# Quartered products for the 16- and 32-row tiles of a pooling and recurrence decoder layer

## What is computed

```python
def _layer(x, pool_prev, S0, start_pos, prompt, lb, ...):
    h = _rmsnorm(x, g_mix)
    z = h @ w_in                                   # 1024 -> 4608
    u, q, f, v, og, ga, gb = jnp.split(z, offs, axis=-1)
    pooled = _pool_mix(u_cat, pos)                 # trailing means, windows 2/4/8/16
    ya = (grouped(pooled, w_pool) * pool_scale) @ w_a
    qh = silu(q); fg = lb + (1 - lb) * sigmoid(f); kh = 1 - fg; gh = log(fg)
    # gated recurrence, per head: S_t = diag(fg_t) S_{t-1} + kh_t outer v_t, o_t = S_t^T qh_t
    o = _rmsnorm(o, g_onorm) * silu(og)
    yb = o @ w_b
    m = sigmoid(ga) * ya + sigmoid(gb) * yb
    x = x + m @ w_out
    h2 = _rmsnorm(x, g_mlp)
    x = x + jnp.square(relu(h2 @ w_up)) @ w_down   # 1024 -> 4096 -> 1024
# and y = _rmsnorm(x, g_final); 16 meta tokens stand ahead of each prompt and are dropped from y
```

## Time and profile before

| | |
|---|---|
| median of 3 runs | 899.56 us (899.15 to 900.22) |
| profiled execution: its time, and its span on the slowest core | 899.98 us, 898.4 us |
| spans of the eight cores | 894.7 to 898.4 us |
| mean granted TensorE clock | 0.996 to 0.999 |
| TensorE matmuls busy | 866.9 us, 96% of the span |
| VectorE, ScalarE, GpSimd busy | 418.2, 354.4, 122.1 us |

### The profile page before, as it was taken

The page is one execution under the profiler, slowest core; times in us unless marked ns, Lnnn a source line. Parts: engine busy times, 40 slices in busy tenths (PEclk is TensorE's granted clock), DMA queues, the critical chain, the costliest instruction groups (busy, mean ns, idle before and its releaser), DMA issues.

```text
span 898.4 us, 14902 instructions; the slowest of 8 cores (894.7 to 898.4 us)
## 1 busy us (share of the span) xinstructions
PE 866.9 (96%) x4864; PEld 449.6 (50%) x4945; DVE 418.2 (47%) x695; ACT 354.4 (39%) x625; POOL 122.1 (14%) x190
## 2 busy tenths in 40 slices
PE   4999999999999999999999999999999999999996
PEld 2667654444444444465444444444444444688443
DVE  4574565777487676754544114441144412234122
ACT  3654536564465627541333313332233312233222
POOL 4113320244004511243000000000000000000000
PEclk9999999999999999999999999999999999999999
DMA  9999952448414768978999042200420011200121
GB/s 173 163 169 197 185 144 102 124 120 192 165 47 136 177 192 177 171 106 121 217 204 181 7 137 80 63 1 24 117 94 0 1 47 48 74 1 1 34 67 67
DMA packets 91463, 97.24 MB, mean 108 GB/s; under 512 B 37725, under 2 KB 72157, under 8 KB 91372
## 3 DMA queue, kind: packets, MB, share of 16 engines
q1 hardware_dynamic: 67404, 65.88, 25.7%
q0 software_dynamic: 23984, 30.41, 23.9%
HBM read 92.35 MB, written 26.11 MB: 132 GB/s over the span
## 4 chain that ended last, share of the span: by engine, by line
PE 86%; DVE 4%; issue 4%; ACT 4%; DMA 1%; POOL 0%; DVEq 0%; ACTq 0%; SPq 0%; POOLq 0%
PE ps L595 48%; PE ps L1357 24%; PE ps L607 8%; ACT arena L573 3%; PE ps L1054 2%; DVE arena L576 1%; DVE arena L676 1%; DVE arena L696 1%; DMA arena<-xp 1%; PE ps L621 1%; PE ps L1246 1%; PE ps L906 0%; PE ps L762 0%; PE ps L779 0%; PE ps L1355 0%
## 5 line engine op out<-in xcount | busy, mean ns | idle before, releaser
L595 PE MATMUL ps<-arena 128*128 128x512 bf16 (+2 forms) x2675 | 489.8, 338 | 7.0 <-ACT arena L573 2.4
L595 PEld LDWEIGHTS ps<-arena 128*128 128x128 bf16 x2720 | 261.0, 98 | 211.9 <-issue 16.0
L573 ACT ACTIVATE arena<-ps 128x512 f32<-128x512 f32 (+7 forms) x318 | 185.8, 597 | 293.7 <-PE ps L595 205.9
L573 ACT ACTIVATE arena<-arena 128x1024 bf16<-128x1024 f32 (+6 forms) x234 | 152.2, 666 | 243.4 <-DVE arena L1371 167.6
L1357 PE MATMUL ps<-arena 128*128 128x512 bf16 x1003 | 220.6, 379 | 1.2 <-issue 0.2
L576 DVE TENSOR_TENSOR arena<-arena 128x512 bf16<-128x512 f32 (+6 forms) x214 | 146.4, 691 | 134.7 <-ACT arena L573 125.6
L1357 PEld LDWEIGHTS ps<-arena 128*128 128x128 bf16 x1024 | 100.0, 98 | 121.4 <-issue 1.3
L576 DVE TENSOR_TENSOR arena<-ps,arena 128x512 f32<-128x512 f32 (+4 forms) x153 | 105.9, 708 | 74.2 <-PE ps L595 17.4
L607 PE MATMUL ps<-arena 128*128 128x512 bf16 (+2 forms) x469 | 106.6, 379 | 0.9 <-issue 0.3
L1371 DVE SCALAR_TENSOR_TENSOR arena<-ps,arena 128x1024 f32<-128x1024 f32 (+2 forms) x18 | 22.0, 1222 | 152.5 <-PE ps L1357 138.2
L576 POOL TENSOR_TENSOR arena<-arena 128x512 f32<-128x512 bf16 (+7 forms) x78 | 77.8, 1004 | 74.7 <-DMA arena<-sth 23.6
(11 more groups left out here) (97 smaller groups left out, 237.1 us busy)
## 6 DMA issues: line engine op xcount, KB each, us to landing
arena<-xp SPq DMA_DIRECT2D x32, 512.0 KB, 6.7
arena<-w_in POOLq DMA_DIRECT2D x9, 1024.0 KB, 20.5
x1d<-arena SPq DMA_DIRECT2D x16, 512.0 KB, 5.2
arena<-w_up POOLq DMA_DIRECT2D x8, 1024.0 KB, 12.7
arena<-x1d SPq DMA_DIRECT2D x16, 512.0 KB, 4.6
y_p<-arena SPq DMA_DIRECT2D x15, 512.0 KB, 2.9
arena<-w_down POOLq DMA_DIRECT2D x5, 1024.0 KB, 25.5
h2d<-arena SPq DMA_DIRECT2D x16, 256.0 KB, 4.6
```

The lines of the kernel that those rows point to most:

```text
L573: P.add("act", lambda h: h.activation(out=out, in_=in_, func=func, **kw), reads=reads, writes=writes)
L595: i = h.matmul(ps[:, bb, 0:m], lhsT=wfn(k), rhs=rfn(k, c, m), start=(k == 0), stop=(k == K - 1))
```

## The change

The three small products go in quarters like the down projection: matmul k writes to partitions 32 (k % 4) and up, so each quarter of the array's columns adds up two of the eight k. The four partial sums then lie in four quarters of the bank's partitions, and VectorE adds them: a copy of the first to SBUF and three additions for v and og, four additions to `X` for the output projection, a copy and three additions for the down projection. ScalarE then reads the sum from SBUF. The down projection's copy by ScalarE and its `sel` matmuls go, and its last steps are no longer put off.

```diff
+        def quarters(lfn, K, rfn, rows, ps_of, nh, wr, rd):
+
+            def mm(h):
+                for k in range(K):
+                    for half in range(nh):
+                        j = 32 * (k % 4)
+                        i = h.matmul(ps_of(half)[j:j + rows], lhsT=lfn(k), rhs=rfn(k, half), start=(k < 4), stop=(k >= K - 4))
+                return i
+            P.add("pe", mm, reads=rd, writes=wr)
...
             def u_tm(blk, t, evac):
                 W = wblk[SLOT[blk]]
                 if t < 0:
-                    tm(lambda k: H[:, k, 0:32], 8, lambda k: W[:, k, :], 32, evac, [bH[4]] + r_w[SLOT[blk]].bufs)
+                    b = banks(1)
+                    quarters(lambda k: H[:, k, 0:32], 8, lambda k, half: W[:, k, :], 32, lambda half: ps[:, b, :], 1, [b_ps[b]], [bH[4]] + r_w[SLOT[blk]].bufs)
+                    for j in range(4):
+                        if j == 0:
+                            P.add("dve", lambda h: h.tensor_copy(out=osq[0:32, :], in_=ps[0:32, b, :]), reads=[b_ps[b]], writes=r_oq.bufs)
+                        else:
+                            tt(osq[0:32, :], ps[32 * j:32 * j + 32, b, :], osq[0:32, :], ALU.add, [b_ps[b]] + r_oq.bufs, r_oq.bufs)
+                    evac(osq[0:32, :], r_oq.bufs)
...
                 X, bX = xi[t]
+                if t == 4:
+                    b = banks(2)
+                    quarters(lambda k: mT[:, k, 512:528], 8, lambda k, hf: wo[:, k, hf * 512:(hf + 1) * 512], 16, lambda hf: ps[:, b + hf, :], 2, b_ps[b:b + 2], r_wo.bufs + r_mT.bufs)
+                    Xv = X[0:16, :].rearrange("p (a n) -> p a n", a=2)
+                    for j in range(4):
+                        tt(Xv, ps[32 * j:32 * j + 16, b:b + 2, :], Xv, ALU.add, b_ps[b:b + 2] + bX, bX)
+                    return
...
                     U(lambda: u_o(t, 0))
-                    U(lambda: u_o(t, 1))
+                    if t < 4:
+                        U(lambda: u_o(t, 1))
...
                 if t == 4:
                     activate(r_cp)
-                    P.add("act", lambda h, b=b: h.activation(out=cp.rearrange("p (a n) -> p a n", a=2), in_=ps[:, b:b + 2, :], func=AF.Copy), reads=[b_ps[b], b_ps[b + 1]], writes=r_cp.bufs)
-
-                    def fin16(out=out, fin=fin):
-                        pb = banks(2)
-
-                        def mm(h):
-                            for half in range(2):
-                                x = h.matmul(ps[0:16, pb + half, :], lhsT=sel, rhs=cp[:, half * 512:(half + 1) * 512], start=True, stop=True)
-                            return x
-                        P.add("pe", mm, reads=r_cp.bufs + [b_pk], writes=[b_ps[pb], b_ps[pb + 1]])
-                        out((0, 1), src=ps[0:16, pb:pb + 2, :], bsrc=[b_ps[pb], b_ps[pb + 1]])
-                        fin(((0, 1024),))
-                    pend.append(fin16)
+                    cv = cp[0:16, :].rearrange("p (a n) -> p a n", a=2)
+                    for j in range(4):
+                        if j == 0:
+                            P.add("dve", lambda h, b=b: h.tensor_copy(out=cv, in_=ps[0:16, b:b + 2, :]), reads=[b_ps[b], b_ps[b + 1]], writes=r_cp.bufs)
+                        else:
+                            tt(cv, ps[32 * j:32 * j + 16, b:b + 2, :], cv, ALU.add, [b_ps[b], b_ps[b + 1]] + r_cp.bufs, r_cp.bufs)
+                    out((0, 1), src=cv, bsrc=r_cp.bufs)
+                    fin(((0, 1024),))
```

More of the change, by code:

```diff
@@ L333, in build_program @@
         gon = pk[:, 316:317]
-        sel = pk[:, 320:336]
         ident_b, (b_idb,) = keep(128, BF16)
@@ L1328, in down @@
             seq = [0, 4, 1, 2, 3] if g == 3 else [0, 1, 2, 3]
-            pend = []
             for n, t in enumerate(seq):
@@ L1360, in down @@
                 x1load(rows_of.index((g, t)) + 1)
-                while pend:
-                    pend.pop(0)()
                 halves = [[Buf("half")], [Buf("half")]]
```

## The result

The changed kernel takes 910.61 us (median of five runs) against 899.93 for the kernel before in the same runs: 1.0116 of it, 95% interval 1.0102 to 1.0129, so 9.2 to 11.6 us slower. 908.9 had been forecast, with 905.0 to 911.8 as the range.

The account below looks back on a forecast made before the run. TensorE, busy 866.9 of 898.4 us, was taken to bound the kernel. Terms 6.4 + 3.0 + 0 - 1.8 + 1.7 = +9.3 us gave 909.3, or 908.9 for the median; range 905.0 to 911.8.

Parts of the forecast that it names:

- the clock term: TensorE's waits at `u_v` and `u_og`: one half-rate stretch of 3.4 us counted in full, +1.7 us, bounds 0 and 3.4.
- place 1: `u_v(-1)`: additions behind `prep_scan(1)` make TensorE wait for the bank and ScalarE for the sum; +6.4 us, bounds 5.7 to 6.9.
- TensorE has no slack to absorb a stall: Whole kernel: TensorE is busy 866.9 of 898.4 us, so any stall or saving on it should show in the total.
- the second wait that I had announced: Before the first `u_u`: TensorE waits about 2 us for ScalarE, after its wait of 5 to 6 us for VectorE.
- Place 2: `u_og(-1)`: additions delay `prep_q(3)`, which the first recurrence tile's products need; +3.0 us, bounds 2.3 to 3.5.
- Place 3: Output projection, tile 4: 2.3 us saved, then lost waiting ahead of `up(0)`'s third unit; 0, bounds -0.5 to +0.5.
- Place 4: Down projection: `sel` matmuls leave TensorE's path and the next tile's 64 matmuls hide the additions; -1.8 us.
- a clock that stays down for longer than one such stretch: Sign the prediction is wrong: half rate lasting longer than one 3.4 us stretch behind TensorE's waits.
- both clock falls in full: Rival inside the forecast's range: half-rate stretches behind both the `u_v` and `u_og` waits, 910.6 us; no separate chance given.
- a stall that doesn't come: Rival: no stall at `u_og(-1)`, as `prep_q(3)` or the chain runs ahead; 905.9 us, or 904.2 without clock loss; chance 0.10.
- is partly absorbed: Rival: much of the delay is given back in later stages; 900 to 904 us, chance 0.05.
- doesn't exist: Rival: VectorE gets to the additions in time at `u_v` and `u_og`; 6.1 us less, 893.5 us, chance 0.04.

Follow-up runs that it names:

- the two runs without ScalarE's wait: Changed kernel with ScalarE's copy of `u_v(-1)`'s sum put off: alone 909.83 us; also with unused matmuls in TensorE's two long waits, 905.28 us.
- the filled waits: Changed kernel with 22 unused matmuls ahead of `u_v(3)` and 15 ahead of the first recurrence tile's products: 906.56 us, ratio 1.0070.

## Why the prediction was right

The direction, the size and the waits behind them were right; the size of the clock term was not, and one point of the account at place 1 held only in part.

*That TensorE has no slack to absorb a stall* held: one at a time, the four places add up to the whole within the noise.

*Place 1, +6.4.* 6.3 by the trace, with the additions where the lists put them. The wait for the bank was 5.45 us (5.5 forecast). The step on ScalarE was only half of the cause: `u_v(3)` at half rate ends at the same moment, and each delay hides the other, as the two runs without ScalarE's wait showed. So the second wait that I had announced, about 2 us for ScalarE, is not in the changed kernel's profile; it came up (1.83 us) when the clock was kept up. The four `u_u` took 0.35 us more behind it.

*Place 2, +3.0.* 3.1 by the trace, and for the reason given: moved behind `prep_q(3)`, the same additions cost none of it. (0.2 of the 3.1 is the clock, since with the waits filled it was 2.9.)

*Place 3, 0.* The wait came (1.98, forecast 2.3), TensorE saved 2.6 where I had 2.3, and 0.4 us was kept; on some cores, four of the changed kernel and one of the kernel with this edit alone, a half-rate stretch behind it took 1.7 us back. The kernel with this edit alone can't be told from the one before.

*Place 4, -1.8.* -1.9 by the trace. Measured alone: -1.7, interval -2.6 to -0.9.

*The clock, +1.7.* That the waits bring it down is shown by the filled waits, and the sign is right; the size is the term furthest off. I had one stretch of 3.4 us in full. There were two, and on the slowest core both were 6.8 us long. Behind the second wait it cost 2.4 us, behind the first 0.35 in the `u_u`: 2.8. I had named a clock that stays down for longer than one such stretch as a sign that the prediction is wrong, and for this term it was. Of the 1.7 us between 908.9 and 910.61, 1.1 is this term, and 0.4 is only that the kernel before took 899.93 us in these runs and not the 899.56 that I started from; the rest is not resolved from noise. With later stretches and smaller parts, the filling was worth 4.1.

*What the steps cost.* A dependent addition started about 0.1 us behind the one before, not 0.17: the chain of four took 38.14 to 41.19, 3.05 us (3.27 forecast), that on 1024 columns 5.18 (5.6). The quartered product of 8 matmuls took 0.55 us, not 1.10, and that of 16 took 0.99, not 1.49. I had put 0.7 us of the 64-matmul product down to the last matmul's way and the change out of quarters. 0.2 of it was the missing record; and I had taken the distance of two matmuls from their loads, 0.048 us, where their own is (3.57 - 0.99) / 48 = 0.054, which makes 0.4 over 64. The fixed part is 3.57 - 64 x 0.054 = 0.1. None of this mattered at the first two places, where TensorE waited anyway.

*The rivals.* The case of both clock falls in full was the closest, 910.6. By it the Trainium skill ("TensorE: Matmul & The Clock Gate", Part 1: an idle array falls to half rate and must be busy for a while to get it back) foretold the total better than my middle value. The trace agrees, with 0.50 granted for 6.8 us behind waits of 5.45 and 4.15 us. That its total was right to a tenth is luck: it priced two stretches at 1.7 us each, and they cost 2.4 and 0.35. The other rivals, a stall that doesn't come, is partly absorbed, or doesn't exist, are out.

## What to carry to other kernels

A cheaper product is only worth it if its eviction can be moved out of the way: look up, in each engine's list, what stands ahead of the new steps and who stands behind them, and what bank or buffer they hold meanwhile; 3 us of additions cost 6.3 us at one place, 3.1 at another, and at that second place next to nothing (0.2) when they were put behind their neighbours. Price a new wait of TensorE with the half-rate stretch behind it, not by its own length alone. And before a product is shortened, check that the stretch in which it lies is TensorE's: at `u_v` the 1.3 us were hardly on the path, while the savings at the output and down projections gave 4 us together once the output projection's sums had banks of their own.

## What the runs showed of the hardware

TensorE's half rate followed its standing: behind waits of 5.45 and 4.15 us all eight cores had a stretch at 0.50, of 3.4 or 6.8 us, and none had one there when the waits were filled with matmuls that nobody needs, which made the kernel 4.1 us faster. A single wait of 1.98 us was followed by a half-rate stretch on some cores and not on others of the same run (8.75 against 6.85 us for nearly the same matmuls). Quartered products of 8, 16 and 64 matmuls took 0.55, 0.99 and 3.57 us, that is 0.054 us for each and 0.1 for the product; whole ones of 8 and 16 took 1.83 and 3.55, 0.216 for each and 0.1 for the product. So going in and out of quarters cost no more than going from one product to the next.
